# Eight weight-block sums per seven-product pair on GpSimd in place of VectorE

## The reference

```python
def swiglu(h, wg, wu, wd):
    return (jax.nn.silu(h @ wg) * (h @ wu)) @ wd
...
for l in range(2):
    h = modulated_norm(x, norm_g[l, 0], sh1, sc1)
    x = x + 0.5 * g1 * swiglu(h, ffn_wg[l, 0], ffn_wu[l, 0], ffn_wd[l, 0])
    ...
    h = modulated_norm(x, norm_g[l, 2], sh3, sc3)
    x = x + 0.5 * g3 * swiglu(h, ffn_wg[l, 1], ffn_wu[l, 1], ffn_wd[l, 1])
```

## Time and profile before

| | |
|---|---|
| median of 3 runs | 2664.66 us (2664.61 to 2665.74) |
| span of the profiled execution | 2663.4 us |
| TensorE busy | 2646.7 us (99%) |
| VectorE busy | 1758.1 us (66%) |
| ScalarE busy | 1087.0 us (41%) |
| GpSimd busy | 71.4 us (3%) |

### The profile page before, as it was taken

One profiled execution on the slowest core, in us unless ns is written; L12 is line 12 of the kernel. 1 busy time (PEld: TensorE's weight loads), 2 busy tenths in 40 slices (PEclk: granted clock), 3 DMA queues, 4 the chain that ended last, 5 costly groups with the idle time before them and its releaser, 6 DMA issues.

```text
span 2663.4 us, 37114 instructions
## 1 busy us (share of the span) xinstructions
PE 2646.7 (99%) x14953; PEld 2315.7 (87%) x14953; DVE 1758.1 (66%) x2177; ACT 1087.0 (41%) x1497; POOL 71.4 (3%) x119
## 2 busy tenths in 40 slices
PE   8999999999999999999999999999999999999999
PEld 7888988888888888888878999989898988898998
DVE  7677563586666765657566776768676654676775
ACT  5555432342223432224465434445353432453433
POOL 1000000000000000000400000000000000000000
PEclk9999999999999999999999999999999999999999
DMA  4211232556565465554312333223233323232332
GB/s 145 64 63 63 70 98 98 187 188 215 201 201 184 138 211 201 201 197 142 95 48 80 111 95 111 81 94 111 95 111 103 104 81 101 88 111 91 115 95 79
DMA packets 257929, 324.33 MB, mean 122 GB/s; under 512 B 5766, under 2 KB 248708, under 8 KB 249604
## 3 DMA queue, kind: packets, MB, share of 16 engines
q1 hardware_dynamic: 245904, 245.12, 28.9%
q0 software_dynamic: 9216, 75.50, 7.7%
q10 hardware_dynamic: 2676, 1.84, 0.2%
HBM read 320.34 MB, written 2.10 MB: 121 GB/s over the span
## 4 chain that ended last, share of the span: by engine, by line
PE 98%; ACT 0%; DVE 0%; DMA 0%; ACTq 0%; issue 0%; DVEq 0%
PE po L749 18%; PE po L750 18%; PE po L751 18%; PE po L1123 6%; PE po L1122 6%; PE po L1121 6%; PE po L919 2%; PE pm L949 2%; PE po L921 2%; PE po L920 2%; PE po L818 1%; PE po L820 1%; PE po L833 1%; PE po L861 1%; PE po L866 1%; PE po L852 1%
## 5 line engine op out<-in xcount | busy, mean ns | idle before, releaser
L1504 ACT ACTIVATE w_hi<-w_raw 128x1024 fp32r<-128x1024 f32 x326 | 329.6, 1050 | 567.7 <-PE po L751 529.7
L2284 DVE TENSOR_TENSOR w_lo<-w_raw,w_hi 128x1024 fp32r<-128x1024 f32 x364 | 432.8, 1221 | 176.2 <-ACT w_hi L1504 170.7
L749 PE MATMUL po<-b_hi,w_hi 128*128 128x512 f32 x1008 | 392.8, 390 | 0.0
L750 PE MATMUL po<-b_lo,w_hi 128*128 128x512 f32 x1008 | 392.2, 389 | 0.0
L751 PE MATMUL po<-b_hi,w_lo 128*128 128x512 f32 x1008 | 392.2, 389 | 0.0
L749 PE MATMUL po<-a_hi,w_hi 128*128 128x512 f32 x976 | 380.1, 389 | 0.0
L751 PE MATMUL po<-a_hi,w_lo 128*128 128x512 f32 x976 | 379.7, 389 | 0.0
L750 PE MATMUL po<-a_lo,w_hi 128*128 128x512 f32 x976 | 379.7, 389 | 0.0
L751 PEld LDWEIGHTS po<-b_hi,w_lo 128*128 128x128 f32 x1008 | 189.2, 188 | 39.5
L749 PEld LDWEIGHTS po<-b_hi,w_hi 128*128 128x128 f32 x1008 | 189.2, 188 | 39.0
L750 PEld LDWEIGHTS po<-b_lo,w_hi 128*128 128x128 f32 x1008 | 189.3, 188 | 38.7
(11 more groups left out here) (473 smaller groups left out, 5723.9 us busy)
## 6 DMA issues: line engine op xcount, KB each, us to landing
ada_in<-in_w_ada_dram POOLq DMA_DIRECT2D x64, 1152.0 KB, 5.5
w_raw<-in_ffn_wg_dram SPq DMA_DIRECT2D x44, 1024.0 KB, 5.4
w_raw<-in_ffn_wu_dram SPq DMA_DIRECT2D x44, 1024.0 KB, 5.4
w_raw<-in_w_ff_dram SPq DMA_DIRECT2D x32, 1024.0 KB, 5.2
w_raw<-in_ffn_wd_dram SPq DMA_DIRECT2D x32, 1024.0 KB, 5.0
w_raw<-in_w_in_dram SPq DMA_DIRECT2D x27, 1024.0 KB, 5.1
w_raw<-in_ffn_wd_dram SPq DMA_DIRECT2D x16, 768.0 KB, 4.2
w_raw<-in_w_in_c_dram SPq DMA_DIRECT2D x12, 1024.0 KB, 5.1
```

The costliest lines, as they stand in the source:

```text
L749: pe.matmul(o, wh, hi[:, k, :], start=(k == ks[0]), stop=False)
L750: pe.matmul(o, wh, lo[:, k, :], start=False, stop=False)
L1504: act.activation(w_hi[:, s, part], w_raw[:, s, part], ACT.Copy).then_inc(hi_done, 1)
L2284: dve.tensor_tensor(w_lo[:, s, part], w_raw[:, s, part], w_hi[:, s, part].bitcast(F32), ALU.subtract).then_inc(lo_done, 1)
```

## The change

block_sum and all its calls leave VectorE's list. GpSimd gets the eight sums of every pair, in the order s3g, s2g, s4g, s1g, s3u, s2u, s4u, s1u, pair after pair, at the end of its list. Two waits are new there: s2 of a pair waits for the "lo" of batch 3 of the pair before (stats is still read), and, in the first pair of a swiglu, for the end of the norm, which uses stats too. The other orders stay, with the sums taken out.

```diff
+            def block_sum(step, l, j, g, i):
...
+                if step[:2] == "s3":
+                    pool.wait_ge(s_x_dve[s], x_dve[s].after("lo", w))
...
+                elif step[:2] == "s2":
+                    pool.wait_ge(s_x_sum, x_sum.after("s3" + c, w))
+                    if w:
+                        pool.wait_ge(s_x_dve[2], x_dve[2].after("lo", w - 1))
+                    if g == 0 and i == PLAIN_PAIRS:
+                        pool.wait_ge(s_n_dve, norm_dve[f"{l}{2 * j}"].after(f"t{DK - 1}b"))
...
+                pool.tensor_tensor(out_, a, b, op).then_inc(s_x_sum, x_sum.one(step))
+
+            for l, j in SEVEN:
+                for g, n in enumerate(GROUPS):
+                    for i in range(seven_from(l, j, g), n // 2):
+                        for step in SUMS:
+                            block_sum(step, l, j, g, i)
...
                 first_block("u", hid[:, 0:QT])
                 lo(1)
-                total("s3g")
-                total("s2g")
-                total("s4g")
-                total("s1g")
                 lo(2)
-                total("s3u")
                 if head:
                     fourth_block("g", ev[:, 0, 3 * QT:4 * QT])
-                total("s2u")
                 if not head:
                     fourth_block("g", ev[:, 0, 3 * QT:4 * QT])
-                total("s4u")
                 if head:
                     fourth_block("u", hid[:, 3 * QT:4 * QT])
-                total("s1u")
...
                 block_lo(1, l, j, 0, i)
                 block_lo(2, l, j, 0, i)
-                for step in ("s3g", "s2g", "s4g", "s1g", "s3u", "s2u"):
-                    block_sum(step, l, j, 0, i)
                 block_lo(4, l, j, 0, i)
-                block_sum("s4u", l, j, 0, i)
-                block_sum("s1u", l, j, 0, i)
                 block_lo(6, l, j, 0, i)
...
                 if v == 3:
-                    block_sum("s1u", l, j, g, 0)
                     block_lo(3, l, j, g, 0)
                     return
...
+                for batch in (1, 2, 4, 6):
+                    block_lo(batch, l, j, g, 0)
```

More of the change, by code:

```diff
@@ L354, in hybrid_two_block_kernel @@
         s_x_dve = [sem(f"block_lo_dve{b}") for b in range(1, 6)]
-        s_x_sum = sem("block_sums_dve")
+        s_x_sum = sem("block_sums_pool")
         s_y_act, s_y_dve, s_y_pe = sem("seven_act"), sem("seven_dve"), sem("seven_pe")
@@ L448, in hybrid_two_block_kernel @@
         x_dve = [Steps(s_x_dve[b], ["lo"], reps=n_seven) for b in range(5)]
-        x_sum = Steps(s_x_sum, [f"s{m}{c}" for c in "gu" for m in (3, 2, 4, 1)], reps=n_seven)
+        SUMS = ("s3g", "s2g", "s4g", "s1g", "s3u", "s2u", "s4u", "s1u")
+        x_sum = Steps(s_x_sum, SUMS, reps=n_seven)
         y_act = Steps(s_y_act, ["u1g", "u1u", "u2g", "u2u", "u3g", "u3u", "silu21", "silu22", "silu1"], reps=n_seven)
@@ L722, in _ @@
                     .then_inc(s_win, win_pool.one(f"pf{g}"))
+            def block_sum(step, l, j, g, i):
+                w = SEVEN_FIRST[l, j, g] + i
+                c = step[-1]
+                s = "gu".index(c)
+                if step[:2] == "s3":
+                    pool.wait_ge(s_x_dve[s], x_dve[s].after("lo", w))
+                    out_, a, b, op = raw_block(s, 0, 0), raw_block(s, 0, 0), raw_block(s, 1, 0), ALU.subtract
+                elif step[:2] == "s2":
[4 more added lines that the diff above has]
+                        pool.wait_ge(s_n_dve, norm_dve[f"{l}{2 * j}"].after(f"t{DK - 1}b"))
+                    out_, a, b, op = sum_block(s), raw_block(s, 1, 1), raw_block(s, 0, 0), ALU.subtract
+                elif step[:2] == "s4":
+                    pool.wait_ge(s_x_sum, x_sum.after("s2" + c, w))
+                    out_, a, b, op = raw_block(s, 0, 1), raw_block(s, 0, 1), sum_block(s), ALU.subtract
+                else:
+                    pool.wait_ge(s_x_sum, x_sum.after("s3" + c, w))
+                    out_, a, b, op = raw_block(s, 1, 0), raw_block(s, 1, 0), raw_block(s, 1, 1), ALU.add
+                pool.tensor_tensor(out_, a, b, op).then_inc(s_x_sum, x_sum.one(step))
[4 more added lines that the diff above has]
+                            block_sum(step, l, j, g, i)
         @block.tensor
@@ L2912, in block_lo @@
                     ins.then_inc(lo_done, 2)
[L2914 to L2931, removed]
             def raw_sums(l, j):
@@ L2999, in lo @@
                         block_lo(batch, l, j, g, i + 1)
-                def total(step):
-                    if more:
-                        block_sum(step, l, j, g, i + 1)
                 def first_block(c, out_):
```

## The result

The changed kernel takes 2766.95 us (2764.89 to 2768.96, 4 runs) against 2665.2 before (2664.61 to 2665.99, 4 runs): a ratio of 1.038, with a 95% interval of 1.037 to 1.0395, or +101.8 us. Forecast were 2780, a range of 2712 to 2835, and slower with 0.95.

The account below looks back on a forecast made before the run. TensorE was taken to bound the kernel, so only its new stalls count: per block 10.6 + 16.0 + 11.7 (groups 0, 1, 2) = 38.3 us, times three +115, 2664.7 to 2780 us; range 2712 to 2835.

Parts of the forecast that it names:

- TensorE is the whole path, relief of VectorE is worth nothing: Pair stages: TensorE busy throughout at the upper clock; taking 149 us of sums off VectorE gains 0.
- A sum costs 1.29: GpSimd's price per 128x512 sum running alone, 1.29 us against 0.69 on VectorE; 1.04 as the lower end.
- Exclusion: GpSimd operations and VectorE operations with two SBUF inputs exclude each other; together 20.4 us in a 20.16 us pair.
- The loop of 24.5 us: From one lo(1) to the next in later pairs: 24.5 us, so +4.3 us per pair once it binds.
- Group 0: 5.6 and 5.0: First group of each block: opening pair loses 5.6 us, the pair behind it about 5.0 at c11g; together 10.6.
- Group 1: 3.7, 7.3, 4.3, 0.7: Four pairs: first loses 3.7 us, second 3.75 plus 3.55, third 4.3, last 0.7 at c11g; together 16.0.
- the tie between two queues: If GpSimd always wins against a waiting subtraction, chains move 1.2 us either way, about +-20 us over all.
- rival d: TensorE's clock falls after some six stalls above 3 us per block: +20, 2800 us; chance 0.15.
- Rival a: Sums on GpSimd cost nearer 1.04 us: 2738 us; chance 0.22 including what lies between, 2715 to 2760.
- Rival b: No exclusion that matters, sums 1.29 us: about 6.7 us per block, +20, 2685 us; chance 0.09.
- Rival c: Sums take 1.04 us and don't exclude the subtractions; p4u loses 0.5 us at most: 2664 to 2668; chance 0.04.
- Rival e: Worse sums or worse queueing than walked: 2820 us and above; chance 0.14.

Follow-up runs that it names:

- spare sums: Kernel before, sums still on VectorE, plus a spare 128x512 subtraction on GpSimd behind each of the 216 sums, awaited by nobody: 2802.8 us, ratio 1.051.
- memsets: Kernel before, sums still on VectorE, plus three 128x512 memsets on GpSimd behind each of the 216 sums: 2665.53 us, ratio 1.000.
- the filler: Changed kernel plus 24 extra matmuls ahead of TensorE's wait for c11g in each group's second pair and the opening pairs: 2763.12 us, ratio 1.037.
- memset chain: Changed kernel with each GpSimd sum replaced by a chain of memsets of its output, all waits kept: 2694.67 us, ratio 1.0118.

## Why the prediction was right

The direction, the mechanism and the size within 14 us: +115 was forecast, +102 came. That the size came so near is in part luck, because three misses pull against one another: the exclusion was priced too high, the bare chain too low, and the clock, which did slow products, had no term in the sum. Step by step:

- **TensorE is the whole path, relief of VectorE is worth nothing.** Right: all of the span's +100 is waits (65.5) and slower products (34.5) at TensorE in the pair stages.
- **A sum costs 1.29.** Right to 0.01.
- **Exclusion.** Right, and shown apart from the chain by the spare sums and the memsets. Its price was too high: the prediction has 115 with it and 20 without, so 95 for it; the runs have 102 and 29.5, so 72. By the rule of the Trainium skill (SBUF — State Buffer, "SBUF: two separate sides"), which holds against a GpSimd operation only if that one reads SBUF, the memset run had to stay at 2665: the trace agrees, no subtraction above 1.226 us.
- **The loop of 24.5 us.** Measured 23.9: 12.4 for the sums (forecast 12.9), 2.1 for hi(5) and hi(6), 1.4 for lo(6), 5.7 until hi(1), 2.3 for hi(1) and lo(1).
- **Group 0: 5.6 and 5.0.** The opening pair took 25.78 us, +5.6, the forecast number, but not its parts: p1u lost 1.0 for 1.4 and p6g 3.0 for 3.3, and 1.6 us of products at the lower clock made up the rest; they covered the next product's wait of 0.9, which appears with the filler (0.8). Its successor lost 6.2: 3.7 at p6g, the rest at the lower clock.
- **Group 1: 3.7, 7.3, 4.3, 0.7.** Measured +2.1, +6.2, +3.75, +0.6. The largest miss is the first, 2.1 for 3.7: s1u ended 4.9 us after the pair's start, not 6.8. VectorE ran lo(4) and lo(6) with one sum between them and s1u (1578.56 to 1579.83) went ahead of lo(3), which took 2.21 us for it. That is the tie between two queues that the prediction named as open.
- **Sum.** Group 2, by its pair starts, lost 2.1 + 7.5 + 0.3. A block lost 11.8 + 12.7 + 9.9 = 34.4 where 10.6 + 16.0 + 11.7 = 38.3 was forecast; three give 103; the span has 100, since the second pair of group 2 lost 7.5 in (0, 1) but only 6.2 in the two other blocks. Group 0 lost more than forecast and groups 1 and 2 less.
- **The clock (rival d).** It did fall, and a third of the loss is read as slow products; the prediction had named that as a sign of being wrong. But it was hardly an addition: in group 1's second pair the forecast stall of 3.55 at p4u was 0.17, and 2.5 us of slow products stood in its place. The filler run turned them back. The reason given, that the loop has no TensorE in it, was right there; adding 20 us for the clock would have been wrong, about 4 came back. In the pairs of (0, 1) that I compared, the clock added only in group 0, where the group ends. Nor did it fall behind every stall above 3 us: behind the 3.1 us at p4u in group 1's third pair the granted clock is 1.00 (1644.5 to 1647.4), and so it is behind the 3.5 us at p6g in the second pair of group 2 of (0, 1) (1743.2 to 1746.5); there the lower level comes behind the next stall, 2.7 us at p4u. By the rule of the Trainium skill (TensorE: Matmul & The Clock Gate, "The HAM clock gate") an idle array falls back to half rate: the trace agrees, with 0.50 granted behind the stall at 1606.32, but the rule doesn't say what that costs.
- **The other rivals.** Rival a (1.04 a sum) falls with the measured 1.29, and shifting an input didn't bring 1.04 either. Rival b is the memset chain and was worth 29.5, not 20: its trace shows 2.2 us in the opening pair and 1.3 in the pair behind it, which the walk had put near nothing, 3.9 in group 1's second pair for 1.9, and only 0.3 in the third, where 1.9 was put as well. Rival c needed both a cheap sum and no exclusion, and had neither. Rival e (worse than walked) did not come: the loss was smaller than walked.

The runs point to no version faster than the kernel before: TensorE had no gap in the pairs to give back, and each part of the sums left on VectorE only brought the time nearer to 2665.

## What to carry to other kernels

Before work goes to an idle GpSimd, look at what VectorE does at that moment. If VectorE's operations read two operands from SBUF and GpSimd's read SBUF, they take turns: add their times on one line instead of two, and count the sums left on VectorE too. Then write down the loop that the moved steps are part of, from buffer freed to buffer freed, and compare it with TensorE's period; when the loop is longer, exchanges in the queue orders or a saved clock may only move the wait, as they did here. A share of 3% for an engine says that it is free, not that what it shares with VectorE is.

## What the runs showed of the hardware that I had not expected

- Memsets of 128x512 on GpSimd, 648 of them in one run, lengthen no subtraction (the longest of w_lo<-w_raw took 1.226 us), while as much time in sums lengthens the longest of the same row to 2.09 (spare sums) and 2.15 (changed kernel).
- The granted clock fell to the lower level behind the stall of 3.4 us in group 1's second pair, and a block product then took 2.56 to 2.69 us for 1.44; 24 matmuls into an unused bank kept it up there. It did not fall behind the 3.5 us stall in the second pair of group 2 of (0, 1).
- GpSimd's sum costs 1.293 us for 512 columns, 1.256 for 496 with a shifted input, 0.74 for 256. The 1.04 us of the pooling sums is not explained by the shift.
